# A decoder step with a routed expert stage: register loads moved from chunk to expert, and a reordered router tail

## The chip, the cores and the metric

One core of one Trainium2 chip runs the whole program. The metric is the device time of one execution in microseconds (us). The core has a matrix engine (PE, with its weight loads listed as PEld), VectorE (DVE), ScalarE (ACT), GpSimd (POOL), SyncE (SP), which here only issues transfers, and 16 DMA engines. Each engine has an instruction sequencer of its own, which also runs loops and register instructions; the engines meet at semaphores.

## What is computed

One layer of a decoder trunk for 512 prompt tokens and 8 sample tokens (520 in all, width 1024): a mixer of four head groups, an output projection with a residual, and then a mixture of experts, top 4 of 32. Only this last part matters here:

```python
logits = x @ wr + br                          # (520, 32)
top_v, top_e = lax.top_k(logits, 4)
gate = softmax(top_v)
# rows are sorted by expert; each expert's rows are padded to whole blocks
for each block of rows of expert e:
    gt, up = split(x[rows] @ wgu[e] + bgu[e], 2)
    gt, up = min(gt, 7), clip(up, -7, 7)
    out = ((up + 1) * gt * sigmoid(1.702 * gt)) @ wd[e] + bd[e]
y[token] = sum over its 4 experts of gate * out
```

## The kernel before

The program is a row of blocks, each closed by a barrier of all engines: front, RWKV, attention, `block_out_router` (L2106), `block_experts` (L2423) and `block_combine` (L2650). The change touches the router block and the expert block.

**The tail of the router block.** Tokens lie on 128 partitions in NR = 5 tiles t, experts (E = 32) along the free axis. VectorE finds the four best logits of each token (L2346 to L2353) as one-hot rows `oh[k]`, sums them to `T1` (L2357 to L2360, one row of 32 per token and tile), then makes the softmax gates and the dense gate matrix `Gd` (L2361 to L2369). It releases PE with the semaphore `rv`. PE then makes the rank of each token within each expert: for tile t it sums `ones` times the T1 of all earlier tiles and `strict` (a strictly triangular matrix) times the T1 of its own (L2240 to L2243, 15 products), then the counts (`ones` times all five T1, L2245, five products), then transposes of `Gd` (L2248, five). Each such f32 product stands as two records in the profile. PE answers with `rp`. VectorE copies the transposed gates to `GT` (L2372, L2373), compares the counts with multiples of SLOTS = 32 to get each expert's number of chunks (L2376 to L2380), sums them up to the first chunk of each (L2383), and writes both as int32 rows into `tab` (L2384 to L2387). It turns ranks into slot numbers (L2389 to L2394), splits each into chunk and place (L2395 to L2398) and builds two one-hot sets, `LO` (times the token number) and `HI` (L2402 to L2405). PE multiplies them, the slot product (L2251 to L2256, 160 records on 32-column weights, four side by side), and VectorE writes the token of each slot into `rowtok` (L2408, L2409). Every VectorE instruction here waits for the one before it.

**The expert block.** Each expert's tokens are worked off in chunks of 32. There are 79 chunks in this run and 32 experts, 2.5 chunks an expert. SyncE streams the weights (per expert 8 MB gate-up in four transfers, L2453, and 4 MB down in two, L2461) into two buffers, b = 0 and 1, in turn. A transfer for expert e+2 waits until PE has used the same part of the buffer in the last chunk of expert e. PE runs a loop over pairs of experts (L2581, `i`), in it the two experts (b), in it a loop over the chunks (L2585, `j`). One chunk (L2553) is: gate-up products of bank 0 and then bank 1 (L2527, 128 records; after half of bank 1, the hidden transposes of bank 0, L2540), `load_next`, the transposes of the next chunk's tokens (L2514), the hidden transposes of bank 1 (L2540), and the down products (L2549, 64 records in two halves). ScalarE copies each gate-up bank out of PSUM before it is transposed (`gs`, L2595); VectorE adds the bias and makes the activation after it (L2625 to L2634), and the two halves of the down product wait for its results. GpSimd gathers the tokens of later chunks and stores rows.

`load_next(e)` (L2576) reads two int32 words of `tab` (first chunk and number of chunks of the next expert) from SBUF into registers of PE's sequencer:

```python
def load_next(e):
    nc.regs_mov(entry[0], pe.value_load(tab[0:1, 0, ds(e, 1)], ...))
    nc.regs_mov(entry[1], pe.value_load(tab[0:1, 1, ds(e, 1)], ...))
```

The old chunk calls it each time (L2561), though the words stay the same within an expert; `F0` and `N` are copied from these registers at the expert's head (L2583, L2584).

Of the kernel before, what the change touches and what calls it, by code (L numbers as in the profile page):

```python
# [16 lines left out]
ALU = mybir.AluOpType  # L17
ACT = mybir.ActivationFunctionType
AX = mybir.AxisListType
# [4 lines left out]
SEQ, DEC = 512, 8  # L24
NTOK = SEQ + DEC
# [4 lines left out]
E, TOPK, FF = 32, 4, 1024  # L30
# [2066 lines left out]
SLOTS = 32  # L2097
MAX_CH = (NTOK * TOPK + E * SLOTS) // SLOTS
MAX_N = -(-NTOK // SLOTS)
SHIFT = 5  # L2100
# [5 lines left out]
def block_out_router(nc, io, G, ctx, sem, sbt):  # L2106
# [19 lines left out]
    h_ok, t_mm, t_ev, l_mm, x1_st, b_mm = (sem("r_" + n) for n in (  # L2126
        "h_ok", "t_mm", "t_ev", "l_mm", "x1_st", "b_mm"))
    h2_st = [sem("r_h2_st0"), sem("r_h2_st1")]
    x1_ok, g_cst, a_ok, rv, rp, ra = (sem("r_" + n) for n in ("x1_ok", "g_cst", "a_ok", "rv", "rp", "ra"))

    strict = sbt(ctx, "strict", [128, 128])
    ioti = sbt(ctx, "ioti", [128, 128], I32)
# [8 lines left out]
    col = sbt(ctx, "col7", [128, NR])  # L2141
    T1 = sbt(ctx, "T1", [128, NR, E])
    Gd = sbt(ctx, "Gd", [128, NR, E])
    thr = sbt(ctx, "thr", [128, E, MAX_N])
    nch = sbt(ctx, "nch", [128, E])
    one_e = sbt(ctx, "one_e", [128, E])
# [10 lines left out]
    def rows_of(t):  # L2157
        return 128 if t < NT else DEC

    with nc.Block() as block:  # L2160
# [29 lines left out]
        @block.tensor  # L2190
        def _(pe):
            def out_proj_sample():
                for a in range(2):
                    pe.wait_ge(w_o_in[a], 16)
                for k in range(KD):
                    for q in range(4):
                        m = pe.matmul(ps[32 * q:32 * q + DEC, 0, 0:256], mixT[:, k, SEQ:NTOK],
                                      w_out[:, k, q * 256:(q + 1) * 256], start=(k == 0), stop=(k == KD - 1))
                m.then_inc(o_mm, 1)

            def out_proj(s):
                t = order[s]
                r = rows_of(t)
                if s >= 2:
                    pe.wait_ge(o_rd, s - 1)
                for a in range(2):
                    for k in range(KD):
                        m = pe.matmul(ps[0:r, 2 * (s % 2) + a, :], mixT[:, k, t * 128:t * 128 + r],  # L2208
                                      w_out[:, k, a * 512:(a + 1) * 512], start=(k == 0), stop=(k == KD - 1))
                m.then_inc(o_mm, 1)  # L2210

            def router(s):
                t = order[s]
                r = rows_of(t)
                pe.wait_ge(h_ok, s + 1)
                if s >= 1:
                    pe.wait_ge(t_ev, s)
                for k in range(KD):
                    m = pe.transpose(ps[:, 4 + k // 4, (k % 4) * 128:(k % 4) * 128 + r],
                                     h2[0:r, s % 2, k * 128:(k + 1) * 128], ident[0:r, 0:r])  # L2220
                m.then_inc(t_mm, 1)
                pe.wait_ge(t_ev, s + 1)
                for k in range(KD):
                    m = pe.matmul(ps[0:r, 6, t * E:(t + 1) * E], h2T[:, s % 2, k, 0:r], wr[:, k, :],
                                  start=(k == 0), stop=(k == KD - 1))
                m.then_inc(l_mm, 1)

            out_proj_sample()
            out_proj(1)
            pe.wait_ge(w_in_, 48)  # L2230
            for c in range(2 * FF // 128):
                m = pe.transpose(ps[:, 7, c * E:(c + 1) * E], bgu[:, c * 128:(c + 1) * 128], ident[0:E, 0:E])
            m.then_inc(b_mm, 1)
            for s in range(NR):
                router(s)
                if s + 2 < NR:
                    out_proj(s + 2)

            pe.wait_ge(rv, 1)
            for t in range(NR):  # L2240
                for j in range(t + 1):
                    m = pe.matmul(ps[:, 0, t * E:(t + 1) * E], (strict if j == t else ones)[:], T1[:, j],
                                  start=(j == 0), stop=(j == t))  # L2243
            for j in range(NR):
                m = pe.matmul(ps[:, 1, 0:E], ones[:], T1[:, j], start=(j == 0), stop=(j == NR - 1))  # L2245
            for t in range(NR):
                r = rows_of(t)
                m = pe.transpose(ps[0:E, 2 + t // 4, (t % 4) * 128:(t % 4) * 128 + r], Gd[0:r, t], ident[0:r, 0:r])  # L2248
            m.then_inc(rp, 1)
            pe.wait_ge(rv, 2)  # L2250
            for k in range(TOPK):  # L2251
                for t in range(NR):
                    for c in range(BLK):
                        m = pe.matmul(ps[SLOTS * c:SLOTS * c + SLOTS, 4, 0:MAX_CH], LO[:, k, t], HI[:, k, t],
                                      start=(k == 0 and t == 0), stop=(k == TOPK - 1 and t == NR - 1))
            m.then_inc(rp, 1)  # L2256

        @block.scalar
        def _(act):
# [32 lines left out]
        def _(v):  # L2292
# [65 lines left out]
            for k in (2, 3):  # L2358
                L(TT(T1[:], T1[:], oh[:, k], ALU.add))
            L(TT(T1[:], T1[:], e_(valid[:]), ALU.mult))  # L2360
            v.wait_ge(ra, 1)  # L2361
            L(v.tensor_reduce(col[:], tops[:].rearrange("p k t -> p t k"), AX.X, ALU.add))
            L(v.reciprocal(col[:], col[:]))
# [3 lines left out]
            for k in (1, 2, 3):  # L2367
                L(TT(tmp[:], oh[:, k], e_(tops[:, k]), ALU.mult))
                L(TT(Gd[:], Gd[:], tmp[:], ALU.add))  # L2369
            v.sem_inc(rv, 1)  # L2370
            v.wait_ge(rp, 1)
            L(v.tensor_copy(GT[:, 0:512], ps[0:E, 2, :]))  # L2372
            L(v.tensor_copy(GT[:, SEQ:NTOK], ps[0:E, 3, 0:DEC]))  # L2373

            cnt = ps[:, 1, 0:E]
            L(v.tensor_scalar(thr[:], iot[:, 0:MAX_N].unsqueeze(1).broadcast_to((128, E, MAX_N)),  # L2376
                              float(SLOTS), None, ALU.mult))
            L(TT(thr[:], thr[:], cnt.unsqueeze(2).broadcast_to((128, E, MAX_N)), ALU.is_lt))
            L(v.tensor_reduce(nch[:], thr[:], AX.X, ALU.add))
            L(v.tensor_scalar(nch[:], nch[:], 1.0, None, ALU.max))  # L2380
            L(v.memset(one_e[:], 1.0))
            L(v.memset(firstc[:, 0:1], 0.0))
            L(v.tensor_tensor_scan(firstc[:, 1:E + 1], one_e[:], nch[:], 0.0, ALU.mult, ALU.add))  # L2383
            L(v.tensor_copy(tab[0:1, 0, 0:E + 1], firstc[0:1]))  # L2384
            L(v.tensor_copy(tab[0:1, 1, 0:E], nch[0:1]))
            L(v.memset(tab[0:1, 1, E:E + 2], 1))
            L(v.tensor_scalar(tab[0:1, 0, E + 1:E + 2], firstc[0:1, E:E + 1], -2.0, None, ALU.add))  # L2387
            L(v.tensor_scalar(nch[:], firstc[:, 0:E], float(SLOTS), None, ALU.mult))
            L(TT(T1[:], ps[:, 0, 0:NR * E].rearrange("p (t e) -> p t e", e=E),  # L2389
                 nch[:].unsqueeze(1).broadcast_to((128, NR, E)), ALU.add))  # L2390
            for k in range(TOPK):
                L(TT(tmp[:], oh[:, k], T1[:], ALU.mult))
                L(v.tensor_reduce(slotf[:, k], tmp[:], AX.X, ALU.add))
            L(v.tensor_copy(slot_i[:], slotf[:].rearrange("p k t -> p t k")))  # L2394
            L(v.tensor_copy(part[:, 0], slotf[:]))  # L2395
            L(v.tensor_scalar(part[:, 1], part[:, 0], SLOTS - 1, None, ALU.bitwise_and))
            L(v.tensor_scalar(part[:, 0], part[:, 0], SHIFT, None, ALU.arith_shift_right))
            L(v.tensor_copy(partf[:], part[:]))  # L2398
            L(TT(tokf[:], tokf[:], valid[:], ALU.mult))
            kt = lambda x: x.rearrange("p k t b -> p (k t) b")  # L2400
            pf = lambda i, n: partf[:, i].rearrange("p k t -> p (k t)").unsqueeze(2).broadcast_to((128, TOPK * NR, n))
            L(TT(kt(LO), iot[:, 0:SLOTS].unsqueeze(1).broadcast_to((128, TOPK * NR, SLOTS)), pf(1, SLOTS), ALU.is_equal))  # L2402
            for k in range(TOPK):
                L(TT(LO[:, k], LO[:, k], tokf[:].unsqueeze(2).broadcast_to((128, NR, SLOTS)), ALU.mult))
            L(TT(kt(HI), iot[:, 0:MAX_CH].unsqueeze(1).broadcast_to((128, TOPK * NR, MAX_CH)), pf(0, MAX_CH), ALU.is_equal))  # L2405
            v.sem_inc(rv, 1)
            v.wait_ge(rp, 2)
            L(v.memset(rowtok[:, MAX_CH:MAX_CH + AHEAD], 0))  # L2408
            L(v.tensor_scalar(rowtok[:, 0:MAX_CH], ps[:, 4, 0:MAX_CH], float(BLK), blkf[:, 0:1], ALU.mult, ALU.add))  # L2409

# [10 lines left out]
def block_experts(nc, io, G, ctx, sem, sbt):  # L2423
# [20 lines left out]
    with nc.Block() as block:  # L2444
# [66 lines left out]
        def _(pe):  # L2511
# [41 lines left out]
            def chunk(b, i, g):  # L2553
# [3 lines left out]
                for q in range(NQ):  # L2557
                    gate_up(1, q, b, i, g)
                    if q == 1:
                        turn_hidden(0, g)  # L2560
                load_next(2 * i + b + 1)  # L2561
                pe.wait_ge(x_in, 16 * g + 32)
                pe.sem_inc(pe_go, 1)
                turn_tokens()
# [16 lines left out]
            with pe.Fori(0, E // 2) as i:  # L2581
                for b in range(2):
                    F0 = pe.snap(entry[0], min_val=0, max_val=MAX_CH - 1)  # L2583
                    N = pe.snap(entry[1], min_val=1, max_val=MAX_N)  # L2584
                    with pe.Fori(0, N) as j:  # L2585
                        chunk(b, i, F0 + j)

# [188 lines left out]
```

## Time and profile before

| | us |
|---|---|
| three timed runs | 2397.13, 2416.45, 2417.66 (median 2416.45) |
| the profiled execution | 2398.06, its span 2396.4 |
| router block's tail, last logits to barrier | 1154.7 to 1200.1 |
| expert block | 1200.1 to about 2309 |
| combine | to 2396.4 |

In the profile a time is counted from the span's start. An engine's idle time is put down to what ended it ("<-"); "issue" means that nothing shown by the profile released the engine. A PE matmul's end is modelled; successive matmuls overlap, so starts are the better measure. Records of a sequencer carry a "q" behind the engine's name.

### The profile page before, as it was taken

What the parts mean: (1) busy time and instruction counts of PE and PEld (TensorE: products, weight loads), DVE (VectorE), ACT (ScalarE), POOL (GpSimd) and SP (SyncE); (2) the same over time, 40 slices, a digit from 0 to 9 for tenths busy, and PEclk for the clock granted to TensorE, in tenths of its full rate; (3) what the DMA queues carried; (4) which work ended last, traced back from release to release, by engine and by line L of the source; (5) the groups of instructions that cost most, each with busy time, mean ns of one, the idle gap of its engine ahead of it and who ended that gap; (6) DMA issues with size and microseconds to landing.
All of it is one profiled execution on the core that took longest, in us unless ns stands there. A gap on an engine that the chain in (4) does not pass through costs nothing. (4 is left out here: it accounts for less than half of the span.)

```text
span 2396.4 us, 53953 instructions
## 1 busy us (share of the span) xinstructions
PE 1844.4 (77%) x21694; PEld 1235.2 (52%) x21695; DVE 862.7 (36%) x2159; ACT 322.0 (13%) x754; POOL 265.9 (11%) x504
## 2 busy tenths in 40 slices
PE   5999358438887688749379986997989999998651
PEld 4887258335444377724345543554556655655320
DVE  3000865514665622336522221221222222222128
ACT  1000201004322211200011110111111111111000
POOL 0000100041000220000011110110111111111030
PEclk9999579658555755879589998998999999999775
DMA  9720000061400000362099999999999198997982
GB/s 318 240 92 22 12 10 1 2 235 53 193 1 1 1 36 12 131 235 117 18 385 413 411 413 414 392 382 413 411 413 403 62 412 321 412 397 309 414 315 85
DMA packets 131717, 533.48 MB, mean 223 GB/s; under 512 B 19292, under 2 KB 35697, under 8 KB 97123
## 3 DMA queue, kind: packets, MB, share of 16 engines
q1 hardware_dynamic: 110092, 474.92, 50.2%
q0 software_dynamic: 19952, 56.76, 6.2%
q8 instruction: 51, 0.84, 0.2%
q10 hardware_dynamic: 1600, 0.79, 0.1%
q14 instruction: 22, 0.18, 0.0%
HBM read 509.46 MB, written 24.95 MB: 223 GB/s over the span
## 5 line engine op out<-in xcount | busy, mean ns | idle before, releaser
L2527 PE MATMUL ps<-wgu,xTm 128*32 128x256 f32 x10112 | 611.1, 393 | 73.2 <-DMA wgu<-in_moe_wgu 71.8
L2527 PEld LDWEIGHTS ps<-wgu,xTm 128*32 128x32 f32 x10112 | 377.1, 113 | 267.0 <-issue 125.9
L2549 PE MATMUL ps<-wd,aT 128*32 128x256 f32 x5056 | 306.5, 382 | 17.4 <-DMA wd<-in_moe_wd 13.8
L2625 DVE TENSOR_TENSOR hx<-ps,biasT 128x256 f32<-128x256 f32 x158 | 67.1, 425 | 604.6 <-PE ps L2540 604.6
L2549 PEld LDWEIGHTS ps<-wd,aT 128*32 128x32 f32 x5056 | 163.4, 109 | 135.4 <-issue 66.7
L314 PE MATMUL ps<-hT,w_ring 128*128 128x260 f32 (+2 forms) x768 | 172.8, 386 | 2.0 <-DVE hT L356 2.0
L314 PEld LDWEIGHTS ps<-hT,w_ring 128*128 128x128 f32 (+2 forms) x768 | 140.6, 184 | 32.4 <-issue 4.9
L2595 ACT ACTIVATE gs<-ps 128x256 f32<-128x256 f32 x158 | 60.7, 384 | 642.2 <-PE ps L2527 642.2
L2483 POOL COPY gidx<-rowtok 128x1 int32 (+1 forms) x79 | 14.4, 183 | 858.3 <-PE ps L2514 858.3
L2645 DVE COPY orow<-ps 128x256 f32 x79 | 33.5, 424 | 201.3 <-PE ps L2549 201.3
L2599 ACT ACTIVATE sg<-hx 128x128 f32<-128x128 f32 x158 | 48.9, 310 | 281.7 <-DVE hx L2627 281.7
L2479 POOL DMA_INDIRECT xg<-h_dram,gidx x79 | 78.8, 998 | 64.7 <-POOL gidx L2483 64.7
L2540 PE MATMUL ps<-ident,gs 128*128 128x128 f32 x316 | 67.4, 295 | 0.0
L684 PE MATMUL ps<-par_buf 128*128 128x128 f32 (+1 forms) x480 | 59.7, 286 | 7.6 <-DVE par_buf L947 5.6
L1368 PE MATMUL ps<-ident,P 128*128 128x128 f32 x120 | 35.8, 417 | 35.8 <-DVE P L1500 30.4
L2490 POOL DMA_DIRECT2D outbuf<-orow x79 | 59.8, 757 | 24.6 <-DVE orow L2645 12.2
L684 PEld LDWEIGHTS ps<-par_buf 128*128 128x128 f32 x480 | 57.5, 199 | 9.5 <-DVE par_buf L947 6.5
L2514 PE MATMUL ps<-ident,xg 128*128 128x128 f32 x160 | 33.0, 288 | 35.0 <-issue 25.2
L2208 PE MATMUL ps<-w_out_s,mixT 128*128 128x512 f32 x128 | 59.5, 625 | 0.0
L1382 PE MATMUL ps<-PTt,rowsV 128*64 128x128 f32 x240 | 58.0, 401 | 0.0
L1368 PEld LDWEIGHTS ps<-ident,P 128*128 128x128 f32 x120 | 18.7, 196 | 74.2 <-DVE P L1500 49.0
L1796 PE MATMUL ps<-ident,cache 128*64 128x128 f32 x272 | 52.1, 356 | 5.9 <-DMA cache<-in_cache_dsa_kv,blk_idx 5.9
(607 smaller groups left out, 2165.0 us busy)
## 6 DMA issues: line engine op xcount, KB each, us to landing
wgu<-in_moe_wgu SPq DMA_DIRECT2D x128, 2048.0 KB, 24.6
wd<-in_moe_wd SPq DMA_DIRECT2D x64, 2048.0 KB, 32.3
ada_ring<-in_w_ada SPq DMA_DIRECT2D x12, 2048.0 KB, 12.7
w_ring<-in_w_in SPq DMA_DIRECT2D x10, 1024.0 KB, 5.4
outbuf<-orow POOLq DMA_DIRECT2D x79, 128.0 KB, 8.4
outbuf<-zD SPq DMA_DIRECT2D x8, 512.0 KB, 8.7
w_out_s<-in_w_out SPq DMA_DIRECT2D x2, 2048.0 KB, 10.4
xh<-in_x_prompt SPq DMA_DIRECT2D x1, 2048.0 KB
```

The costliest lines, as they stand in the source:

```text
L314: mm = pe.matmul(ps[0:w, b + a, 0:HALF], w_ring[:, n % RING_IN, k, i * 128:i * 128 + w], hT[:, k, a * HALF:(a + 1) * HALF], start=(k == 0) ...
L684: m = pe.matmul(ps[:, out_bank, h * w:(h + 1) * w], lhs(h), rhs(h), start=True, stop=True)
L1368: m = pe.transpose(ps[:, 2 + u % 2, k * 128:(k + 1) * 128], P[:, u % 3, k * 128:(k + 1) * 128], ident[:])
L1382: m = pe.matmul(o, rowsV[:, b, k, HD:128], PT[:, u % 2, k * 128:(k + 1) * 128], start=(k == 0 and b == DSA), stop=(last and k == i))
L2208: m = pe.matmul(ps[0:r, 2 * (s % 2) + a, :], mixT[:, k, t * 128:t * 128 + r], w_out[:, k, a * 512:(a + 1) * 512], start=(k == 0), stop=(k ...
L2479: nc.gpsimd.indirect_dma_start(xg[:], None, h_rows, bass.IndirectOffsetOnAxis(ap=idx, axis=0))\
L2490: pool.dma_start(rows4(G["outbuf"][ds(c * SLOTS, SLOTS), :]), orow[:, ds((c & 1) * 256, 256)]).then_inc(r_st, 16)
L2527: m = pe.matmul(ps[32 * c:32 * c + 32, p, 0:256].rearrange("r (s n) -> r s n", s=2), xT[:, t, 32 * q:32 * q + 32], wgu[b][:, 2 * q + t, :, ...
L2540: m = pe.transpose(ps[:, 2 + p, s * 128:(s + 1) * 128], gs[:, p, s * 128:(s + 1) * 128], ident[:])
L2549: m = pe.matmul(ps[32 * c:32 * c + 32, 6, 0:256], aT[:, k, :], wd[b][:, k, 256 * c:256 * c + 256], start=(k == 0), stop=(k == KD - 1))
L2595: nc.scalar.activation(gs[:, p, :], ps[:, p, 0:256], ACT.Copy).then_inc(gu_ev, 1)
L2625: TT(h, ps[:, 2 + p, 0:256].rearrange("p (a n) -> p a n", a=8), b, ALU.add).then_inc(t_rd, 1)
```

## The change

In the router block, a new tile `ahead` holds running sums of T1 over the tiles: `ahead[0]` = 0, `ahead[t+1]` = `ahead[t]` + T1[t], so that its sixth row is the sum over all tiles. Two wide products take the place of the 20 narrow ones: `ones` times `ahead` (192 columns) and `strict` times T1 (160 columns), added up in one bank, whose last 32 columns are the counts. Some of VectorE's work that doesn't need the ranks is done before it waits for them. The gates and `Gd` are made after the operands of the slot product are released; PE transposes `Gd` after the slot product, under two new semaphores, `rg` and `rgt`, and the copies to `GT` are VectorE's last instructions. In the expert block, `load_next` moves from the chunk to the expert's head.

```diff
@@ block_out_router, PE
             pe.wait_ge(rv, 1)
-            for t in range(NR):
-                for j in range(t + 1):
-                    m = pe.matmul(ps[:, 0, t * E:(t + 1) * E], (strict if j == t else ones)[:], T1[:, j],
-                                  start=(j == 0), stop=(j == t))
-            for j in range(NR):
-                m = pe.matmul(ps[:, 1, 0:E], ones[:], T1[:, j], start=(j == 0), stop=(j == NR - 1))
-            for t in range(NR):
-                r = rows_of(t)
-                m = pe.transpose(ps[0:E, 2 + t // 4, (t % 4) * 128:(t % 4) * 128 + r], Gd[0:r, t], ident[0:r, 0:r])
-            m.then_inc(rp, 1)
+            pe.matmul(ps[:, 0, 0:(NR + 1) * E], ones[:], ahead[:].rearrange("p t e -> p (t e)"), start=True, stop=False)
+            pe.matmul(ps[:, 0, 0:NR * E], strict[:], T1[:].rearrange("p t e -> p (t e)"), start=False, stop=True)\
+                .then_inc(rp, 1)
             pe.wait_ge(rv, 2)
...
             m.then_inc(rp, 1)
+            pe.wait_ge(rg, 1)
+            for t in range(NR):
+                r = rows_of(t)
+                m = pe.transpose(ps[0:E, 2 + t // 4, (t % 4) * 128:(t % 4) * 128 + r], Gd[0:r, t], ident[0:r, 0:r])
+            m.then_inc(rgt, 1)
@@ block_out_router, VectorE
             L(TT(T1[:], T1[:], e_(valid[:]), ALU.mult))
+            L(v.memset(ahead[:, 0], 0.0))
+            for t in range(NR):
+                L(TT(ahead[:, t + 1], ahead[:, t], T1[:, t], ALU.add))
+            v.sem_inc(rv, 1)
+            L(v.tensor_scalar(thr[:], ...))
+            L(v.memset(one_e[:], 1.0))
+            L(v.memset(firstc[:, 0:1], 0.0))
+            L(TT(tokf[:], tokf[:], valid[:], ALU.mult))
+            v.wait_ge(rp, 1)
+            cnt = ps[:, 0, NR * E:(NR + 1) * E]
+            L(TT(thr[:], thr[:], cnt..., ALU.is_lt))
...
+            L(TT(kt(HI), ..., pf(0, MAX_CH), ALU.is_equal))
+            v.sem_inc(rv, 1)
+            L(v.tensor_copy(tab[0:1, 0, 0:E + 1], firstc[0:1]))
+            L(v.memset(tab[0:1, 1, E:E + 2], 1))
+            L(v.tensor_scalar(tab[0:1, 0, E + 1:E + 2], firstc[0:1, E:E + 1], -2.0, None, ALU.add))
+            L(v.tensor_copy(slot_i[:], slotf[:].rearrange("p k t -> p t k")))
             v.wait_ge(ra, 1)
             L(v.tensor_reduce(col[:], tops[:].rearrange("p k t -> p t k"), AX.X, ALU.add))
...
                 L(TT(Gd[:], Gd[:], tmp[:], ALU.add))
-            v.sem_inc(rv, 1)
-            v.wait_ge(rp, 1)
-            L(v.tensor_copy(GT[:, 0:512], ps[0:E, 2, :]))
-            L(v.tensor_copy(GT[:, SEQ:NTOK], ps[0:E, 3, 0:DEC]))
...
+            v.sem_inc(rg, 1)
             v.wait_ge(rp, 2)
             L(v.memset(rowtok[:, MAX_CH:MAX_CH + AHEAD], 0))
             L(v.tensor_scalar(rowtok[:, 0:MAX_CH], ...))
+            v.wait_ge(rgt, 1)
+            L(v.tensor_copy(GT[:, 0:512], ps[0:E, 2, :]))
+            L(v.tensor_copy(GT[:, SEQ:NTOK], ps[0:E, 3, 0:DEC]))
@@ block_experts, PE
                         turn_hidden(0, g)
-                load_next(2 * i + b + 1)
                 pe.wait_ge(x_in, 16 * g + 32)
...
                     N = pe.snap(entry[1], min_val=1, max_val=MAX_N)
+                    load_next(2 * i + b + 1)
                     with pe.Fori(0, N) as j:
                         chunk(b, i, F0 + j)
```

## Rows read from the trace of the kernel before

**Rows 1.** The page's first line.

```profile
span 2396.4 us, 53953 instructions
```

**Rows 2.** Stages: us, busy us (instructions) by engine, PE clock, DMA share, GB/s.

```profile
core 0: us, PE busy (x) PEld busy (x) DVE busy (x) ACT busy (x) POOL busy (x), PEclk, DMA share, GB/s
1140.00:1200.10 60.10, 21.36 (x229) 19.98 (x229) 34.06 (x96) 2.73 (x4) 0.00 (x0) 0.52 0.05 18
1200.10:1502.30 302.20, 251.32 (x3934) 148.67 (x3935) 69.38 (x219) 37.13 (x102) 40.23 (x62) 0.92 1.01 410
...
1796.70:1914.50 117.80, 114.50 (x1913) 71.53 (x1913) 31.80 (x100) 16.34 (x46) 17.46 (x27) 1.00 0.59 232
...
2026.90:2171.30 144.40, 140.36 (x2310) 86.96 (x2310) 38.76 (x122) 19.88 (x56) 21.34 (x33) 0.99 0.91 366
```

**Rows 3.** Timeline of the router's tail: start, length, engine, line, operation [idle before].

```profile
1165.84 0.33 DVE L2360 TENSOR_TENSOR T<-T,valid 128x160 f32<-128x160 f32 x1
...
1178.23 1.16 PE L2248 MATMUL ps<-ident,Gd 128*32 128x128 f32 x5
...
1180.81 0.72 DVE L2378 TENSOR_TENSOR thr<-thr,ps 128x544 f32<-128x544 f32 x1
...
1193.06 6.05 PE L2254 MATMUL ps<-w_out_s 128*32 128x97 f32 x160 [13.67 <-DVEq L2406]
...
1199.31 0.32 DVE L2409 TENSOR_SCALAR rowtok<-ps,blkf 128x97 int32<-128x97 f32 x1
```

**Rows 4.** Line L2577's register loads: count, duration min/median/max ns, first and last start.

```profile
L2577 PEldq TENSOR_LOAD <-tab x79: 296/302/329, 1219.4 to 2295.1; - x79
```

**Rows 5.** Sequencer records of one chunk, 1829 to 1831.5: load's first step, next instruction.

```profile
L2577 PEldq FUSED_REGOPS  x3: 59/60/151, 1829.1 to 1829.9; - x3
...
L2563 PEldq EVENT_SEMAPHORE  x1: 51/51/51, 1830.8 to 1830.8; - x1
```

**Rows 6.** Timeline behind the load in two chunks: ScalarE's copy, token and hidden transposes.

```profile
1401.94 0.39 ACT L2595 ACTIVATE gs<-ps 128x256 f32<-128x256 f32 x1 [0.68 <-PE ps L2527]
...
1402.21 0.41 PE L2514 MATMUL ps<-ident,xg 128*128 128x128 f32 x2 [0.34 <-issue]
...
1402.47 0.41 PE L2540 MATMUL ps<-ident,gs 128*128 128x128 f32 x2
...
1416.49 0.39 ACT L2595 ACTIVATE gs<-ps 128x256 f32<-128x256 f32 x1 [0.68 <-PE ps L2527]
...
1416.71 0.41 PE L2514 MATMUL ps<-ident,xg 128*128 128x128 f32 x2 [0.28 <-issue]
...
1417.02 0.41 PE L2540 MATMUL ps<-ident,gs 128*128 128x128 f32 x2
```

**Rows 7.** PE timeline: starts of four chunks; heads at 1342.27 (b=0) and 1366.79 (b=1).

```profile
1329.82 5.39 PE L2527 MATMUL ps<-wgu,xTm 128*32 128x256 f32 x96
...
1342.27 5.39 PE L2527 MATMUL ps<-wgu,xTm 128*32 128x256 f32 x96
...
1354.53 5.39 PE L2527 MATMUL ps<-wgu,xTm 128*32 128x256 f32 x96
...
1366.79 5.39 PE L2527 MATMUL ps<-wgu,xTm 128*32 128x256 f32 x96
```

**Rows 8.** Line L2453, issue to landing of one transfer: issued 1761.1, then 1570.2.

```profile
DMA to landing us min/median/max: 9.1/9.1/9.1
...
DMA to landing us min/median/max: 7.5/7.5/7.5
```

**Rows 9.** VectorE groups of the router block: count, busy us, mean ns, idle before.

```profile
L2404 DVE TENSOR_TENSOR w_out_s<-w_out_s,tokf 128x160 f32<-128x160 f32 x4 | 1.3, 325 | 0.1
...
L2380 DVE TENSOR_SCALAR nch<-nch 128x32 f32<-128x32 f32 x1 | 0.2, 180 | 0.0
```

**Rows 10.** PE timeline: the five products that make the counts, ten records.

```profile
1176.10 2.32 PE L2245 MATMUL ps<-T,ones 128*128 128x32 f32 x10
```

**Rows 11.** PE timeline: gate-up products behind a wait for weights.

```profile
1786.43 2.80 PE L2527 MATMUL ps<-wgu,xTm 128*32 128x256 f32 x48 [2.49 <-DMA wgu<-in_moe_wgu]
...
1938.43 4.48 PE L2527 MATMUL ps<-wgu,xTm 128*32 128x256 f32 x48 [2.15 <-DMA wgu<-in_moe_wgu]
```

## What is predicted

> **What bounds the kernel now.** I read the page first, for the span: 2396.4 us [rows 1]; the profiled execution took 2398.06, so 1.7 us lie around it. The three timed runs are 2397.13, 2416.45 and 2417.66. With the profiled one that makes four times in two pairs, some 19 us apart, and one trace cannot show what parts them. The sum is made against 2398.06; the pairs come back at the end.
>
> Second, the table of stages [rows 2], where the reader is to see the DMA share beside the PE's busy time. Up to 1200.1 us, in the tail of the router block, the DMA engines are idle (0.05) and VectorE has most of the work. So this tail is on the path with its full length: SyncE's first expert weights can't start before the block's barrier. From there to 1502.3 the weights stream without a break (share 1.01), and a late PE is absorbed by the waits that it has for weights anyway. Later there are four stretches in which it is the other way round, and the two longest are shown: the share falls to 0.59 and 0.91, and the PE is busy for nearly all of the time (114.50 of 117.8 us). There the DMAs wait for the PE to free a weight buffer, and whatever makes the PE later makes the end later.
>
> Third, the timeline of the router's tail [rows 3], for the order and the distances. Fourth, the sequencer's records of the table load [rows 4, 5] and the timeline around it [rows 6], which tell what the load costs where it stands. Fifth, chunk starts around an expert's head [rows 7] and the landing times of weights [rows 8], which tell what it costs where it goes.
>
> **The router part.** Old order: T1 is complete at 1166.17 (1165.84 + 0.33); then VectorE makes the gates; PE runs ranks and counts up to 1178.2 and five transposes until 1179.39; two GT copies and the threshold table come next, and only at 1180.81 does the comparison with the counts start. The slot product starts at 1193.06, and the last instruction ends at 1199.63 [rows 3]. New order, in steps:
> - After T1 come one memset and five additions on 128x32. The nearest row is 180 ns [rows 9]; with some 35 ns from one to the next that is 5 x 0.215 + 0.15 = 1.2 us. The ranks are released at 1167.4.
> - Two wide products replace 20 narrow ones (40 records). No row has their shape. The slot product moves 160 records of 97 columns in 6.05 us, four of them side by side [rows 3], so 151 ns a record and 1.56 ns a column at the same low clock; 2 records of 192 and 2 of 160 columns are 1.1 us. With 0.4 for the last record's way through (a pair of transpose records takes 0.41 from start to end, [rows 6]) and 0.1 for the semaphore I take 1.6, nearer to the columns alone (1.1) than to the upper bound of 2.3 (ten old records, [rows 10]). The counts stand at about 1169.1. VectorE's fillers (thresholds, two memsets, tokf: about 0.9 us) end earlier and are hidden behind the PE.
> - So the comparison starts 11.7 us earlier. From it to the slot product took 12.25 us; out of that stretch go two memsets, three table writes, slot_i and tokf, 1.15 us at the size of the small row [rows 9]. The slot product starts at 1180.2, 12.9 earlier, and ends at 1186.3.
> - Behind it something is added: the transposes (1.16) and the two GT copies (0.9) now come after the slot product, about 2.2 us with their handovers, less the 0.4 that rowtok took alone. The gates themselves (seven operations of 0.325, four of 0.19, and table writes: some 4.1 us, [rows 9]) fit under the 6.05 of the slot product; without that cover they would cost 4.1. The block ends at 1188.4 instead of 1199.63.
>
> Gain: 11.3 us, bounds 10 to 12. All later transfers start that much earlier.
>
> **The table load: what is removed.** Each of the 79 chunks makes two loads of 302 ns [rows 4] with register work. The sequencer reaches the first step at 1829.1 and the next instruction behind it at 1830.8 [rows 5], so 1.7 us in all; most of that lies under its lead over the array, which idles 0.28 to 0.34 us before the token transposes [rows 6]. It looks as if 79 x 0.3 could be saved. But the gate is elsewhere: the hidden transposes right behind wait for ScalarE's copy of the second bank. The token transposes start after an idle 0.34 in one chunk and 0.28 in the other, yet the hidden transposes start 0.14 after the end of ScalarE's copy in both (1402.33 to 1402.47, 1416.88 to 1417.02) [rows 6]. The load's jitter does not reach them. That copy hangs on the last gate-up product, and the down product's second half on VectorE's chain behind the transposes. So I cost the removal at nothing; its cover is the copy. Were that cover gone, it would be worth the idle, about 0.33 a chunk.
>
> **What is added.** At an expert's head nothing of that kind covers the sequencer. Inside an expert a chunk follows after 12.26 us; across a head into b=0 after 12.45 [rows 7]: the loop's own register work already outlasts the lead by 0.19. The load comes on top whole, 1.7 us. Into b=1 the crossing takes 12.26, so some lead is left; I take 0.3 and so 1.4. Bounds: 0 (all inside the lead) and 1.7. The whole next chunk is queued behind it.
>
> Only heads inside the PE-bound stretches count, and I follow them in time. 1502 to 1571: the head at 1540.97, 1.7. Up to 1797: the heads at 1694.92 and 1731.86 make the PE 3.1 later than the DMA when it frees a buffer at 1761.1. That transfer landed after 9.1 us because earlier data were still queued; behind an empty queue it takes 7.5 [rows 8], so 1.6 of the 3.1 is covered and 1.5 lost. Later heads before 1797 are absorbed: the PE waits 2.49 on gate-up weights [rows 11] and 2.35 on down weights. There are four joints with two such waits (0.66 to 2.56 each, in sum 4.84, 2.81, 4.28, 4.86); at the second 0.3 of two heads is left over. 1797 to 1914: the head at 1835.20, 1.4. 1949 to 1993: none. 2027 to 2171: the heads at 2055.02, 2091.82 and 2116.53, 4.8. Sum: 1.7 + 1.5 + 1.4 + 0.3 + 4.8 = 9.7 us lost (bounds 0 and 11.5).
>
> The Trainium skill, page "DMA: Bandwidth & Descriptors", section "Latency and other measured facts", gives a tensor_load a floor of about 600 ns. The rows show 302 here, so the trace does not agree, and it decides. By the page a head would cost some 0.6 more (an estimate from it), and the sum would turn out about 4 us worse.
>
> **Sum.** -11.3 + 9.7 = -1.6: the profiled execution's 2398.1 becomes 2396.5.
>
> **Rivals.**
> 1. The load hides at the head too. For it: in a chunk most of it lies under the lead. Against: the 0.19 in [rows 7]. Then only the router part counts: -11.3, 2386.8.
> 2. The chunk does get shorter, by 0.33. For it: the idle in each chunk. Against: the constant 0.14 in [rows 6]. Some 30 chunks lie in PE-bound stretches, -10: with heads at 9.7 that is -11.6 (2386.5), with free heads -21.3 (2376.8).
> 3. Slower: the granted clock falls at the new pauses. After a pause of 2.15 the next 48 products took 4.48 us, after one of 2.49 they took 2.80 [rows 11]; so pauses of this size fall on either side, and the new ones would be about 1.5 to 2. One fall costs 1.68 us; from one at a critical head on the sum is at zero, from the second on the kernel is slower, and with one at each of six it is +8.5, 2406.5. The Trainium skill, page "TensorE: Matmul & The Clock Gate", section "Part 1: The HAM clock gate (the "warmup" mystery)", says that the slow clock is the default and activity lifts it; the trace agrees that falls come behind pauses, not that each pause brings one.
> 4. The wide products don't shorten the ranks. At the old records' pace they would take some 9 us ([rows 10], four times ten) instead of 1.6; the router gains 4, the sum is +5.7, 2403.8.
>
> **How the numbers follow.** Chances: forecast 0.52, rival 1 0.18, rival 2 0.12, rival 3 0.13, rival 4 0.05. About 1% (24 us) is what a measurement of this kernel can tell from no change. No case reaches that against its own base; only rival 2 with free heads comes near, and the two pairs of times can push a median either way. So faster 0.08, same 0.88, slower 0.04. Base for the time is the middle of the four known times, 2407.3; less 1.6 that is 2405.7. The range must hold both pairs: low is the faster pair with rival 1 (2397.6 - 11.3, about 2386), high the slower pair with three clock falls beyond the sum (2417.1 - 1.6 + 5, rounded up to 2422). Within one pair the forecast's own range is -6 to +3.
>
> **What would show it.** Right: slot product near 1180, barrier near 1189; hidden transposes still 0.14 behind ScalarE's copy; chunks inside an expert still 12.26 apart; heads in PE-bound stretches 13.7 to 14.2 apart, with a new pause of 1.5 to 2 us before the first gate-up product. Wrong: heads at 12.3 (rival 1), chunks at 11.9 (rival 2), 48 products of 4.5 us behind heads (rival 3), a comparison that starts after 1171 (rival 4).

## The result, and the profile after

Twenty timed runs of each kernel gave a median of 2416.64 us before and 2397.44 us after; the ratio is 0.9927 with an interval of 0.9900 to 0.9955. Two later comparisons of the same pair gave 1.0028 (0.9993 to 1.0062) and 0.9984 (0.9952 to 1.0017). Executions of either program come in two kinds some 20 us apart, which part ahead of the router block in code that the change leaves alone, and the first ratio leaves out the longer ones of the changed kernel alone, the second those of the kernel before alone and only the third those of both, so what the change itself does is read below from the stages behind that point. There it is worth about -3 us, too little for the whole time to tell. One of the changed kernel's twenty took 5637.28 us; no trace of it was kept, and why is not known.

The table of stages is cut at three marks: the start of the last operation on T1 (L2360 in both kernels), the first expert weight issued, the first instruction of the combine block. Columns as in [rows 2]. The kernel before, router tail and expert block:

```profile
1165.84:1200.12 34.28, 15.77 (x205) 14.92 (x205) 15.98 (x49) 0.00 (x0) 0.00 (x0) 0.53 0.01 1
1200.12:2309.12 1109.00, 977.34 (x15644) 588.76 (x15644) 275.57 (x869) 141.71 (x397) 154.12 (x238) 0.95 0.93 374
```

The changed kernel, the same two stages (span 2414.8 us):

```profile
1185.66:1207.55 21.89, 7.52 (x169) 6.64 (x169) 17.04 (x55) 0.00 (x0) 0.00 (x0) 0.59 0.00 1
1207.55:2327.20 1119.65, 980.00 (x15644) 584.40 (x15644) 275.82 (x869) 138.38 (x397) 154.15 (x238) 0.96 0.92 371
```

The first number behind the window is its length. The tail lost 12.4 us, the expert block gained 10.7. In three profiles of the changed kernel tail and block together are 1141.54, 1139.80 and 1138.83 us, in two of the kernel before 1143.28 and 1142.87: means 1140.1 and 1143.1.

**The router tail.** Timeline of the changed kernel, the answer to [rows 3]:

```profile
1185.66 0.33 DVE L2360 TENSOR_TENSOR T<-T,valid 128x160 f32<-128x160 f32 x1
...
1187.38 1.00 PE L2242 MATMUL ps<-ahead,ones 128*128 128x192 f32 x2 [12.99 <-DVEq L2364]
...
1188.19 0.74 PE L2243 MATMUL ps<-T,strict 128*128 128x160 f32 x2
1189.04 0.72 DVE L2373 TENSOR_TENSOR thr<-thr,ps 128x544 f32<-128x544 f32 x1 [0.69 <-PE ps L2243]
...
1200.10 5.33 PE L2249 MATMUL ps<-w_out_s 128*32 128x97 f32 x160 [11.17 <-DVEq L2394]
...
1204.24 0.33 DVE L2407 TENSOR_TENSOR Gd<-Gd,tmp 128x160 f32<-128x160 f32 x1
1205.35 0.72 PE L2255 MATMUL ps<-ident,Gd 128*32 128x128 f32 x5
...
1206.90 0.15 DVE L2414 COPY GT<-ps 32x8 f32<-32x8 f32 x1
```

The comparison starts 3.38 us behind the T1 row instead of 14.97. The gates end at 1204.57, under the slot product, which ends at 1205.43. Only the transposes, `rowtok` and the two copies to `GT` stick out behind it, until 1207.05.

**The chunk and the head.** Timeline of the changed kernel, PE and ScalarE, the answer to [rows 6] and [rows 7]: the starts of four chunks, of which the head at 1352.03 goes into b=0 and the one at 1377.84 into b=1, and the middle of a later chunk:

```profile
1337.96 5.39 PE L2532 MATMUL ps<-wgu,xTm 128*32 128x256 f32 x96
...
1352.03 5.39 PE L2532 MATMUL ps<-wgu,xTm 128*32 128x256 f32 x96 [1.59 <-issue]
...
1364.29 5.39 PE L2532 MATMUL ps<-wgu,xTm 128*32 128x256 f32 x96
...
1377.84 5.39 PE L2532 MATMUL ps<-wgu,xTm 128*32 128x256 f32 x96 [1.07 <-issue]
...
1411.70 0.44 PE L2519 MATMUL ps<-ident,xg 128*128 128x128 f32 x2
1411.84 0.39 ACT L2600 ACTIVATE gs<-ps 128x256 f32<-128x256 f32 x1 [0.68 <-PE ps L2532]
...
1412.37 0.41 PE L2545 MATMUL ps<-ident,gs 128*128 128x128 f32 x2 [0.23 <-ACT gs L2600]
```

The token transposes follow without a gap now, and the hidden transposes still start 0.14 behind the end of ScalarE's copy (1412.23 to 1412.37). The chunk inside the expert still takes 12.26 (1352.03 to 1364.29). Across a head it takes 14.07 and 13.55, where it was 12.45 and 12.26. The products behind both heads run at full pace, 5.39 us for 96.

The same in the page's groups (line, count, busy us and mean ns, idle before and what ended it). Before, then after:

```profile
L2527 PE MATMUL ps<-wgu,xTm 128*32 128x256 f32 x10112 | 611.1, 393 | 73.2 <-DMA wgu<-in_moe_wgu 71.8 <-ACT xTm L2591 1.3
...
L2514 PE MATMUL ps<-ident,xg 128*128 128x128 f32 x160 | 33.0, 288 | 35.0 <-issue 25.2 <-DMA xg<-h_dram,rowtok 9.8
```

```profile
L2532 PE MATMUL ps<-wgu,xTm 128*32 128x256 f32 x10112 | 602.0, 390 | 89.0 <-DMA wgu<-in_moe_wgu 46.5 <-issue 42.4
...
L2545 PE MATMUL ps<-ident,gs 128*128 128x128 f32 x316 | 67.5, 296 | 18.0 <-ACT gs L2600 18.0
```

This is the change in four numbers. The 25.2 us that the sequencer kept the token transposes waiting are gone, and in their place the hidden transposes wait 18.0 us, by the name of what had held them all along. The loads at the heads show as 42.4 us of waits (3.0 of them in front of the first chunk), but the waits for gate-up weights fall from 71.8 to 46.5: an idle PE only changed the name of its wait wherever the weights were late anyway.

### The profile page after: what moved, and what is told of

Read it like the earlier page. It is cut to its first block and busy times, and to the rows that moved or that the text cites. A ratio compares the mean times of both kernels' runs of the same rounds, so it can differ in the third digit from the quotient of the medians.

```text
span 2414.8 us, 53514 instructions
## 1 busy us (share of the span) xinstructions
PE 1858.4 (77%) x21658; PEld 1240.0 (51%) x21659; DVE 864.1 (36%) x2165; ACT 318.9 (13%) x754; POOL 265.0 (11%) x504
## 5 line engine op out<-in xcount | busy, mean ns | idle before, releaser
L2532 PE MATMUL ps<-wgu,xTm 128*32 128x256 f32 x10112 | 602.0, 390 | 89.0 <-DMA wgu<-in_moe_wgu 46.5
L2545 PEld LDWEIGHTS ps<-ident,gs 128*128 128x128 f32 x316 | 32.1, 142 | 68.5 <-issue 68.5
L1796 PE MATMUL ps<-ident,cache 128*64 128x128 f32 x272 | 60.0, 396 | 5.9 <-DMA cache<-in_cache_dsa_kv,blk_idx 5.9
L1803 PEld LDWEIGHTS ps<-zD,KTs 128*128 128x128 f32 x312 | 58.2, 281 | 10.1 <-issue 10.1
L1803 PE MATMUL ps<-zD,KTs 128*128 128x16 f32 x312 | 62.0, 338 | 0.0
L1797 PE MATMUL ps<-ident,cache 128*64 128x128 f32 x272 | 60.1, 396 | 0.0
## 6 DMA issues: line engine op xcount, KB each, us to landing
w_out_s<-in_w_out SPq DMA_DIRECT2D x2, 2048.0 KB, 10.3
```

The costliest lines, as they stand in the source:

```text
L1796: pe.matmul(out(slice(0, 64)), src[:, t, 2 * j, 0:HD], ident[:], start=True, stop=True)
L1797: return pe.matmul(out(slice(64, 128)), src[:, t, 2 * j + 1, 0:HD], ident[:], start=True, stop=True)
L1803: return pe.matmul(ps[:, t, j * 16:(j + 1) * 16], k, QB[:, q, t], start=True, stop=True)
L2532: m = pe.matmul(ps[32 * c:32 * c + 32, p, 0:256].rearrange("r (s n) -> r s n", s=2), xT[:, t, 32 * q:32 * q + 32], wgu[b][:, 2 * q + t, :, ...
L2545: m = pe.transpose(ps[:, 2 + p, s * 128:(s + 1) * 128], gs[:, p, s * 128:(s + 1) * 128], ident[:])
```

## Experiments

**Each part alone.** The new router tail with `load_next` left in the chunk; and the old tail with `load_next` at the head:

```diff
@@ router_only against the changed kernel: chunk, then the expert's head
                         turn_hidden(0, g)
+                load_next(2 * i + b + 1)
...
                     N = pe.snap(entry[1], min_val=1, max_val=MAX_N)
-                    load_next(2 * i + b + 1)
@@ load_only against the kernel before: chunk, then the expert's head
                         turn_hidden(0, g)
-                load_next(2 * i + b + 1)
...
                     N = pe.snap(entry[1], min_val=1, max_val=MAX_N)
+                    load_next(2 * i + b + 1)
```

> The changed kernel with the two register loads back in every chunk; only the router part is left of the change. Theory A (the load is hidden in the chunk behind ScalarE's copy and exposed at an expert's head): the stretch from T1 to the first expert weight stays at 21.9 us as in the changed kernel (34.3 before), the expert block goes back to 1109.0 us, and the whole is 12.4 us faster than before and some 10 us faster than the changed kernel. Rival B (a chunk pays for its load, so the move is a gain): the expert block is longer than the changed kernel's 1119.7 us, and this kernel is slower than the changed one.

> The kernel before with only the register loads moved to the expert's head. Theory A: expert block 1119.7 us against 1109.0, the whole 10 to 11 us slower than before (ratio 1.004 to 1.005). Rival B: no change or some us faster, up to 0.33 for each of 79 chunks.

Stages of router_only, then of load_only:

```profile
1184.31:1206.58 22.27, 7.93 (x169) 7.05 (x169) 17.02 (x55) 0.00 (x0) 0.00 (x0) 0.57 0.00 1
1206.58:2315.29 1108.71, 975.41 (x15644) 585.86 (x15644) 275.39 (x869) 141.68 (x397) 153.94 (x238) 0.96 0.93 375
```

```profile
1159.90:1194.20 34.30, 15.78 (x205) 14.93 (x205) 15.98 (x49) 0.00 (x0) 0.00 (x0) 0.53 0.00 1
1194.20:2311.12 1116.92, 974.30 (x15644) 582.25 (x15644) 275.64 (x869) 138.03 (x397) 153.95 (x238) 0.97 0.93 372
```

The parts are independent: the tail takes 22.3 or 34.3 by the router part alone, the block 1109 or 1117 by the load alone. The load's move, meant to save work, costs 8 us by itself (10 to 11 had been expected). The ratio of load_only to the kernel before, 1.0116 (1.0060 to 1.0172), is no measure of it: it sets all six executions of load_only, four of them by their times of the longer kind, against those of the shorter kind alone.

**The changed kernel again**, twice:

> The changed kernel once more, for the split of its times. By the stages of the two profiles the change is worth -12.4 in the router's tail, +10.7 in the expert block, -1.4 in all (ratio 0.9994); if the larger step of the medians (0.9927) is the split of the runs in two groups and not the change, runs of the lower group differ by 1 to 5 us and those of the upper one by 0 to 2. If the change itself is worth 17 us, both groups lie 17 us lower than those of before.

> The changed kernel as it is, once more beside the kernel before. What differs by some 20 us between two executions of one program lies ahead of the router block, in code that the change leaves alone. Theory (the change does nothing there): both kernels meet the longer front equally often, and among executions of the same kind the changed kernel is 1 to 3 us shorter; router tail 22, expert block 1118 to 1120. Rival (the changed program meets the longer front less often): at most a third of its executions have it, two thirds of the kernel before, and its median lies some 15 to 20 us lower.

Tail 22.15 and 22.23, block 1117.65 and 1116.60. In after_third's comparison 4 of 23 executions of the kernel before and 3 of 12 of the changed one had the longer front, so there the rival (that the change avoids it) fails, and the medians were 2397.78 and 2395.18, 2.6 apart. In the first comparison, by their times, 14 of 20 and 7 of 20 had it. What sets these shares stays open. What after_again was to show by whole times did not come: sorted by kind, the changed kernel's medians lie 7.6 (lower group) and 0.5 us (upper) under those of the kernel before in the first comparison, but 6.2 above and 6.1 under them in after_again's. So even sorted times scatter by some 7 us and cannot tell 3; that the first ratio owes most of its 0.7% to the shares follows from the stages, not from the times.

> The kernel before once more, for a second profile of it. Router tail 34.3 us and expert block 1109 us within 3 by the theory that the stages behind the router's T1 repeat from run to run; what differs between two profiles of one program lies ahead of the router block, up to 25 us.

Tail 34.38, block 1108.49, and the router block began at 1056.97 where the first profile has 1038.77: these 18.2 us lie ahead of it.

**The two halves of the router part.** wide_only takes the running sums and the two wide products alone; reorder_only takes VectorE's and the transposes' new order with the twenty narrow products. In both the table load stays in the chunk:

```diff
@@ wide_only against the kernel before, PE, then VectorE
-            for t in range(NR):
-                for j in range(t + 1):
...
-                m = pe.matmul(ps[:, 1, 0:E], ones[:], T1[:, j], start=(j == 0), stop=(j == NR - 1))
+            pe.matmul(ps[:, 0, 0:(NR + 1) * E], ones[:], ahead[:].rearrange("p t e -> p (t e)"), start=True, stop=False)
+            pe.matmul(ps[:, 0, 0:NR * E], strict[:], T1[:].rearrange("p t e -> p (t e)"), start=False, stop=True)
...
+            L(v.memset(ahead[:, 0], 0.0))
+            for t in range(NR):
+                L(TT(ahead[:, t + 1], ahead[:, t], T1[:, t], ALU.add))
...
-            cnt = ps[:, 1, 0:E]
+            cnt = ps[:, 0, NR * E:(NR + 1) * E]
```

reorder_only is the kernel before with the rest of the diff of the router block, these lines excepted.

> The kernel before with the running sums and the two wide products alone; VectorE's order, the gates ahead of the release, and the transposes ahead of the comparison stay as they were, the table load stays in the chunk. Theory (the tail is one serial chain, and each part of the change takes its own stretch out of it): six small VectorE operations add 1.2 us, twenty narrow products of 7.8 us become two of 1.7, so the tail from the last operation on T1 to the first expert weight is 34.3 - 4.9 = 29.4 us. Rival (the wide products do nearly all of it): about 23. Other rival (the products don't matter, the gates in front of them do): about 35.5. Expert block 1109 by all.

> The kernel before with VectorE's new order alone: gates, transposes and copies to GT behind the release of the slot product, fillers during the ranks; the twenty narrow products stay, the table load stays in the chunk. Theory (serial chain): the comparison starts about 8.5 us after T1's last operation instead of 15.0 (-6.5), 1.15 of small operations leave the stretch up to the slot product, and 1.8 of transposes and copies are added behind it; the tail is 34.3 - 5.8 = 28.4 us. Rival (the order does nearly all of it): about 23. Other rival (the order only moves the work about): about 34. Expert block 1109 by all.

Timeline of wide_only, then of reorder_only:

```profile
1160.09 0.32 DVE L2357 TENSOR_TENSOR T<-T,valid 128x160 f32<-128x160 f32 x1
...
1165.20 1.01 PE L2241 MATMUL ps<-ahead,ones 128*128 128x192 f32 x2 [16.36 <-DVEq L2370]
1166.00 0.74 PE L2242 MATMUL ps<-T,strict 128*128 128x160 f32 x2
...
1169.13 0.72 DVE L2378 TENSOR_TENSOR thr<-thr,ps 128x544 f32<-128x544 f32 x1
...
1181.38 5.53 PE L2251 MATMUL ps<-w_out_s 128*32 128x97 f32 x160 [13.67 <-DVEq L2406]
```

```profile
1184.31 0.33 DVE L2363 TENSOR_TENSOR T<-T,valid 128x160 f32<-128x160 f32 x1
...
1193.60 0.72 DVE L2373 TENSOR_TENSOR thr<-thr,ps 128x544 f32<-128x544 f32 x1 [7.89 <-PE ps L2246]
...
1204.66 6.15 PE L2252 MATMUL ps<-w_out_s 128*32 128x97 f32 x160 [11.17 <-DVEq L2394]
...
1212.93 0.93 SPq L2466 DMA_DIRECT2D wd<-in_moe_wd  x2
```

| us | T1 to comparison | to slot product | to first weight | tail |
|---|---|---|---|---|
| before | 14.97 | 12.25 | 7.06 | 34.28 |
| wide_only | 9.04 | 12.25 | 6.54 | 27.83 |
| reorder_only | 9.29 | 11.06 | 8.27 | 28.62 |
| after | 3.38 | 11.06 | 7.45 | 21.89 |

In the first two stretches the halves add up: -5.93 and -5.68 make -11.61 (after: -11.59), and 12.25 to 11.06 belongs to the new order alone. In the third they miss by 0.3: -0.52 and +1.21 make +0.69 (after: +0.39). So the tail is one serial chain, and neither half does nearly all of it or nothing, as the rivals had it. Each half has one profile; the tails of the other kernels repeat within 0.6 from profile to profile, and both expert blocks are in place (1108.54 and 1107.48). wide_only saved 6.45 instead of the 4.9 expected: the narrow products had held PE for 8.56 us (1169.67 to 1178.23) instead of the 7.8 that I had put in, and the slot product ran 0.5 faster.

**A second dose at each place.** head_twice makes the load twice at the head; chunk_twice makes it twice in the chunk and not at the head:

```diff
@@ head_twice against the changed kernel, the expert's head
                     load_next(2 * i + b + 1)
+                    load_next(2 * i + b + 1)
@@ chunk_twice against the changed kernel: chunk, then the expert's head
+                load_next(2 * i + b + 1)
+                load_next(2 * i + b + 1)
...
-                    load_next(2 * i + b + 1)
```

> The changed kernel with the two register loads made twice at each expert's head. Theory A: every head is 1.67 us longer again (15.2 us into b=1 and 15.7 into b=0, inside an expert still 12.27), and the expert block grows by the heads on the path, some seven, so by 10 to 13 us to about 1131; the whole is about 10 us slower than before. Rival: the sequencer's lead hides loads at a head, or the DMA's waits absorb them; then the expert block stays within 2 us of 1119.7.

> The changed kernel with the table load put back into the chunk and made there twice instead of once; the router tail is the new one. Theory (in the chunk one load lies under PE's sequencer's lead and ScalarE's copy, and that cover is just used up by one load): the second load's 1.67 us moves the token transposes by as much, and the hidden transposes, which followed 0.26 to 0.31 behind them, by about 1.35. They no longer start 0.14 behind the end of ScalarE's copy but about 1.5. A chunk inside an expert takes 13.6 instead of 12.26 where the PE sets the pace; with some 30 such chunks the expert block is 1109 + 40 = about 1150 us, and more (up to 1185) if further stretches become PE-bound or the granted clock falls. Rival (the cover is ample, a load in a chunk costs nothing at any number): chunks stay at 12.26, the hidden transposes at 0.14, the expert block at 1109 within 3. Router tail 22 us by both.

chunk_twice, timeline of one chunk, PE and ScalarE:

```profile
1357.74 5.39 PE L2532 MATMUL ps<-wgu,xTm 128*32 128x256 f32 x96
...
1365.43 0.38 ACT L2601 ACTIVATE gs<-ps 128x256 f32<-128x256 f32 x1 [0.68 <-PE ps L2532]
1367.06 0.41 PE L2519 MATMUL ps<-ident,xg 128*128 128x128 f32 x2 [1.70 <-issue]
1367.31 0.41 PE L2545 MATMUL ps<-ident,gs 128*128 128x128 f32 x2
...
1371.37 5.39 PE L2532 MATMUL ps<-wgu,xTm 128*32 128x256 f32 x96
```

The hidden transposes start 1.50 behind the end of ScalarE's copy (1365.81 to 1367.31), the chunk takes 13.63, the block 1157.25: 13.6, 1.5 and "about 1150" had been expected. So the first load in the chunk is free only because it just fits under the lead and the copy; there is no room for a second.

head_twice, its expert block, and heads at four places of the timeline:

```profile
1190.11:2344.24 1154.13, 1000.50 (x15644) 592.67 (x15644) 275.51 (x869) 137.83 (x397) 153.71 (x238) 0.94 0.90 360
```

```profile
1233.27 7.07 PE L2532 MATMUL ps<-wgu,xTm 128*32 128x256 f32 x96 [2.55 <-issue]
...
1346.79 7.07 PE L2532 MATMUL ps<-wgu,xTm 128*32 128x256 f32 x96 [2.99 <-issue]
1375.66 5.39 PE L2532 MATMUL ps<-wgu,xTm 128*32 128x256 f32 x96 [2.44 <-issue]
1403.41 5.39 PE L2532 MATMUL ps<-wgu,xTm 128*32 128x256 f32 x96 [3.01 <-issue]
```

The block grew by 36 over the changed kernel's mean of 1118.0, not by the 9 of the first dose; 1131 had been expected, and that is a miss. The heads themselves came nearly as said: 15.46 us into b=0 and 14.92 into b=1 where the pace is full, so a second load costs 1.4 instead of 1.67, and 12.27 inside an expert. But the first two of the heads shown have lost pace, 7.07 us for 96 products where the other two take 5.39: 1.68 more, what one fall of the clock was priced at. The granted clock is 0.76 from 1233.27 to 1240.34 and 1.00 from 1375.66 to 1381.05. Of the 29 heads whose pause the profile puts down to "issue" 17 are slowed so, most by 1.3 to 1.8 us, three by 2.8 to 2.9, and the granted clock of the block is 0.94 instead of 0.96. Pauses of 2.55 and 2.99 brought the fall, 2.44 and 3.01 did not. Where three heads count, from 2042.6 to 2141.1 of the kernel before, head_twice loses 13.4 us and the single load 4.7: some 4.2 of the difference are the second loads and 4.6 two falls (2.90 and 1.68 at heads). The rest of the 36 was not taken apart; more heads count as well, since head_twice is already 6.5 us late at 1528.5, where the changed kernel is not late at all. That is rival 3 of the prediction, at the double dose.

**The better version.** Nothing but the load's move speaks against the change, so router_only was run again beside it:

> The new router tail with the table load left in the chunk, once more and on the same chip as the changed kernel. Theory (the two parts add up, -12.3 and +10): expert block 1109, and among executions of the same kind 12 us shorter than the kernel before and 9 to 11 shorter than the changed kernel. Rival (moving the load is neutral within what can be measured): the same time as the changed kernel within 3.

Tail 21.75, block 1106.93. Among executions without the longer front the medians were about 2397 before, 2394 for the changed kernel and 2387 for router_only. By stages it is 13 us shorter than the kernel before and 10 shorter than the changed one (means 1129.8, 1143.1 and 1140.1). Its ratios by whole times, 1.0009 (0.9960 to 1.0058) and 0.9978 (0.9941 to 1.0015), can't tell it from no change: 13 us is 0.5%, the front moves by more, and both ratios are uneven as that of load_only is. So the better version rests on the stages of two profiles.

## Why the prediction was right, step by step

The forecast was a wash made of -11.3 and +9.7, and so it came: -12.2 and +9.2 as means of the profiles. The kernel is within 1% of the one before, and its median of 2397.4 lies in the range. That it does is no proof, since the range holds both kinds of execution and the predicted time their middle: of the 8.3 us by which the median is under it the stages explain 1.4, and the rest comes of the kind that the median fell on, which is chance.

**Router.** Comparison 11.7 us earlier: it was 11.59. Small operations out of the middle stretch, 1.15: it was 1.19. Wide products 1.6: 1.66 from the first start to the comparison. The one mis-sized term is the stretch from the slot product to the last instruction, 6.95 (1200.10 to 1207.05) instead of 8.2: the slot product took 5.33 instead of 6.05, and the five transposes 0.72 instead of 1.16. The clock shows why. The slot product in the kernel before, then in the changed kernel in two parts:

```profile
1193.00:1199.20 6.20, 6.05 (x160) 5.83 (x160) 0.00 (x0) 0.00 (x0) 0.00 (x0) 0.57 0.01 3
```

```profile
1200.10:1203.80 3.70, 3.70 (x92) 3.70 (x96) 2.88 (x13) 0.00 (x0) 0.00 (x0) 0.50 0.02 7
1203.80:1205.40 1.60, 1.60 (x77) 1.45 (x70) 0.70 (x3) 0.00 (x0) 0.00 (x0) 1.00 0.00 0
```

PE works here without a break; the granted clock is 0.50 in the first part of the changed kernel's slot product and 1.00 in the second (1.2 and 2.4 GHz), and the transposes behind it profit. I had costed both as they stood in the kernel before; there the transposes ran at 0.50 and the slot product at a mean of 0.57, so not wholly "at the same low clock", as the prediction has it. The Trainium skill, page "TensorE: Matmul & The Clock Gate", section "Part 1: The HAM clock gate (the "warmup" mystery)", says that activity lifts the clock; these rows agree.

**Removal at nothing.** Right: 12.26 in every kernel with one load or none in the chunk, the constant 0.14, and chunk_twice as the counter-test. Rival 2 falls.

**The head.** 1.7 into b=0 and 1.4 into b=1 were predicted; 14.07 - 12.45 = 1.62 and 13.55 - 12.26 = 1.29 came. Into b=1 both signs were set a little high: 13.55 lies under the 13.7 to 14.2 that were to show it, and the new pause there is 1.07, not 1.5 to 2. Rival 1 falls. The Trainium skill, page "DMA: Bandwidth & Descriptors", section "Latency and other measured facts", with its floor of about 600 ns for a tensor_load, doesn't agree: the 64 loads at the heads have medians of 310 and 309 ns.

```profile
L2581 PEldq TENSOR_LOAD <-tab x32: 296/310/427, 1217.7 to 2298.9; - x32
```

**Which heads count.** The lag is how much later a chunk starts than the same chunk of the kernel before, both counted from the issue of the first weight (us; the points are the times of the kernel before):

| at | after | after_again | load_only | predicted step, up to this point | measured |
|---|---|---|---|---|---|
| 1528.5 | -0.4 | -0.4 | -0.7 | | |
| 1565.5 | 1.2 | 1.2 | 0.9 | 1.7, head 1540.97 | 1.6 to 1.7 |
| 1798.4 | 3.8 | 4.1 | 3.8 | 1.5, transfer at 1761.1 | 2.6 to 2.9 |
| 1847.5 | 5.0 | 5.4 | 5.2 | 1.4, head 1835.20 | 1.3 to 1.4 |
| 2042.6 | 5.6 | 3.6 | 3.5 | 0.3 left over | +0.6, -1.8, -1.7 |
| 2141.1 | 10.3 | 8.3 | 8.2 | 4.8, three heads | 4.7 |

The third profile, after_third, has the steps 1.6, 2.9, 1.4, -1.8 and 4.8. The heads that I took as exposed cost what was said, and those taken as absorbed disappear (at 1614.7 the lag is 5.6, at 1694.9 again 2.6). Two terms were mis-sized, with opposite signs: the transfer cost 1.1 to 1.4 more than its 1.5, and the joints gave back 1.7 to 1.8 in three of the four profiles instead of costing 0.3. So it is partly luck that 9.2 came so near to 9.7.

The transfer: it was issued 4.2 later, and I let 1.6 of the excess of 3.1 be covered, since its landing could shrink from 9.1 to 7.5 [rows 8]. The first transfer did just that, but the one behind it only went from 13.8 to 13.3, and the next two from 17.4 to 16.9 and from 22.1 to 21.5. Issue to landing of the first two (the median is the mean of the two), in the kernel before, issued at 1761.1 and 1762.0, then in the changed kernel, issued at 1772.8 and 1773.6:

```profile
DMA to landing us min/median/max: 9.1/11.4/13.8
```

```profile
DMA to landing us min/median/max: 7.4/10.4/13.3
```

So the delay passed on is read at the end of the burst, not at its first transfer: the later transfers landed some 3.7 us later of the 4.2.

The joints: I left 0.3 there and did not price the clock behind the waits for weights, although [rows 11] showed it. The kernel before has two waits in the joint that ends at 2029.5, and the products behind the second take longer:

```profile
2016.44 2.80 PE L2527 MATMUL ps<-wgu,xTm 128*32 128x256 f32 x48 [1.72 <-DMA wgu<-in_moe_wgu]
...
2026.90 2.91 PE L2549 MATMUL ps<-wd,aT 128*32 128x256 f32 x32 [2.56 <-DMA wd<-in_moe_wd]
2029.51 4.85 PE L2527 MATMUL ps<-wgu,xTm 128*32 128x256 f32 x69
```

The 69 products take 4.85 us, where the full pace needs some 3.9 (5.39 for 96), and the 32 before them 2.91 instead of 1.93. In the changed kernel PE comes later there, the first wait is gone, the second is shorter, and the clock doesn't fall; at the joint before it does (granted 0.54 over the 3.48 us of the second line):

```profile
1957.42 1.93 PE L2554 MATMUL ps<-wd,aT 128*32 128x256 f32 x32
1961.78 3.48 PE L2554 MATMUL ps<-wd,aT 128*32 128x256 f32 x32 [2.43 <-DMA wd<-in_moe_wd]
...
2041.64 1.93 PE L2554 MATMUL ps<-wd,aT 128*32 128x256 f32 x32 [1.68 <-DMA wd<-in_moe_wd]
```

In after_again the wait at the earlier joint is 1.83, and the 32 products behind it take 1.93. That fall (3.48 - 1.93 = 1.55) is most of the 2.0 that parts the two profiles' blocks, 1119.65 and 1117.65. Both falls lie behind the last wait of their joint, where nothing makes them up. So rival 3's mechanism works at the waits for weights, to both sides, while the new pauses at the heads, 1.06 to 1.94, brought no fall in any of the four profiles of the single load. Rival 4 falls with the wide products' 1.66.

## What to carry to other kernels

A register load that runs in the stream of a busy engine's sequencer may cost nothing, and the same load once per loop head may cost its full length: count not how often an instruction runs, but what covers it where it stands. What a delay costs is decided stretch by stretch, by whether the queue behind it runs dry; here the loads at 32 heads kept PE waiting for some 42 us and the kernel lost 9. A serial tail with idle DMA engines, by contrast, paid back what was taken out of it, and its parts nearly added up.

## What was not expected of the hardware

How the granted clock followed pauses of PE: behind 1.06 to 1.94 us at heads it never fell, behind 2.15 [rows 11] to 3.06 it sometimes did, and a fall mostly cost 1.3 to 1.8 us. So a PE that comes later can get some of it back, since its waits become short (the joint at 2029.5, -1.8). What decides between two pauses of like length stays open. The other surprise is the cover in the chunk: a second load of 1.7 us [rows 5] made the chunk 1.37 longer, so that only 0.3 of it was still hidden.
